# A three-block transformer on one core: projections of the second block from x times feature weights, the norm's factor per token applied later, key heads made once

## The reference

```python
def second_block(x, norm_g, w_in_a, sinks_a, w_in_b, w_out, final_g):
    for i in range(DEPTH_2):                       # 2 layers
        hn = rmsnorm_2(h, norm_g[i])               # x * rsqrt(mean(x^2) + 1e-5) * g
        q, k, v, z = split_proj(hn, w, n_kv)       # 16 query heads of 64; 2 or 4 key heads
        q, k = apply_rope(q, cos, sin), apply_rope(k, cos, sin)
        o = attention(q, k, v)                     # window of 128 with sinks; then causal
        o = o.reshape(B, S, MIX_WIDTH) * jax.nn.silu(z)
        h = h + o @ w_out[i]
    return rmsnorm_2(h, final_g)                   # goes to the third block's first FFN
```

## Time and profile before

| | us |
|---|---|
| runs | 2835.33, 2837.97, 2839.13 (median 2837.97) |
| the profiled execution | 2839.78 |
| its span | 2837.7 |
| PE busy | 2390.9 (84%) |
| DVE busy | 1238.6 (44%) |
| ACT busy | 935.7 (33%) |

### The profile page before, as it was taken

The page is one execution under the profiler, slowest core; times in us unless marked ns, Lnnn a source line. Parts: engine busy times, 40 slices in busy tenths (PEclk is TensorE's granted clock), DMA queues, the critical chain, the costliest instruction groups (busy, mean ns, idle before and its releaser), DMA issues.

```text
span 2837.7 us, 38160 instructions
## 1 busy us (share of the span) xinstructions
PE 2390.9 (84%) x16680; PEld 1711.8 (60%) x16680; DVE 1238.6 (44%) x1752; ACT 935.7 (33%) x1522; POOL 61.2 (2%) x36
## 2 busy tenths in 40 slices
PE   8999998666656565656889899999999999988998
PEld 8897784111211121111678778888788888967787
DVE  5567562000100011000475665467655656845654
ACT  5556541000000000000354554445443453733442
POOL 0000010000000000000000000000000000032000
PEclk9999999778887778777999999999999999999999
DMA  7553468999999999999524255474655554412552
GB/s 237 172 150 118 149 222 368 428 428 428 427 428 427 428 428 428 428 428 428 191 86 138 79 174 193 173 251 165 213 178 193 193 171 154 158 44 77 173 195 92
DMA packets 265894, 698.09 MB, mean 246 GB/s; under 512 B 32352, under 2 KB 208736, under 8 KB 239232
## 3 DMA queue, kind: packets, MB, share of 16 engines
q1 hardware_dynamic: 263424, 681.77, 63.5%
q0 software_dynamic: 2016, 13.67, 1.3%
q10 hardware_dynamic: 288, 0.22, 0.0%
HBM read 694.58 MB, written 1.05 MB: 245 GB/s over the span
## 4 chain that ended last, share of the span: by engine, by line
PE 60%; DMA 30%; DVE 7%; ACT 3%; issue 1%; DVEq 0%; ACTq 0%
PE ps L567 16%; PE ps L569 16%; PE ps L568 16%; DMA af<-in_w_exp_up 14%; DMA af<-in_w_exp_down 7%; DMA af<-in_w_exp_gate 7%; PE ps L1626 2%; PE ps L2396 1%; PE ps L860 1%; PE ps L1145 1%; PE ps L1656 1%; DVE ar L540 1%; PE ps L2016 1%; PE ps L992 1%; PE ps L1158 1%
## 5 line engine op out<-in xcount | busy, mean ns | idle before, releaser
L567 PE MATMUL ps<-ar 128*128 128x512 f32 (+1 forms) x2688 | 941.0, 350 | 28.1 <-DVE ar L1977 6.9
L569 PE MATMUL ps<-ar 128*128 128x512 f32 (+1 forms) x2688 | 923.0, 343 | 0.0
L568 PE MATMUL ps<-ar 128*128 128x512 f32 (+1 forms) x2688 | 922.7, 343 | 0.0
L540 DVE TENSOR_TENSOR ar<-af,ar 128x1024 fp32r<-128x1024 f32 x520 | 612.1, 1227 | 292.0 <-ACT ar L529 291.8
L567 PEld LDWEIGHTS ps<-ar 128*128 128x128 f32 x2688 | 514.5, 191 | 108.3 <-issue 11.8
L529 ACT ACTIVATE ar<-af 128x1024 fp32r<-128x1024 f32 x520 | 516.3, 1049 | 153.2 <-PE ps L569 152.8
L569 PEld LDWEIGHTS ps<-ar 128*128 128x128 f32 x2688 | 514.4, 191 | 59.0
L568 PEld LDWEIGHTS ps<-ar 128*128 128x128 f32 x2688 | 515.1, 192 | 55.7 <-issue 0.5
L1626 PE MATMUL ps<-af 128*32 128x512 f32 x2048 | 331.7, 782 | 220.9 <-DMA af<-in_w_exp_up 117.1
L1626 PEld LDWEIGHTS ps<-af 128*32 128x32 f32 x2048 | 64.3, 127 | 473.1 <-DMA af<-in_w_exp_up 190.7
L1656 PE MATMUL ps<-af 128*32 128x512 f32 x1024 | 163.9, 778 | 99.9 <-DMA af<-in_w_exp_down 87.7
(11 more groups left out here) (284 smaller groups left out, 1665.9 us busy)
## 6 DMA issues: line engine op xcount, KB each, us to landing
af<-in_w_exp_gate SPq DMA_DIRECT2D x64, 2048.0 KB, 41.1
af<-in_w_exp_up SPq DMA_DIRECT2D x64, 2048.0 KB, 40.9
af<-in_w_exp_down SPq DMA_DIRECT2D x64, 2048.0 KB, 41.4
af<-in_ffn_w_in SPq DMA_DIRECT2D x88, 1024.0 KB, 5.8
af<-in_ffn_w_out SPq DMA_DIRECT2D x44, 1024.0 KB, 5.2
af<-in_w_in SPq DMA_DIRECT2D x33, 1024.0 KB, 5.2
af<-in_sgu_w_in SPq DMA_DIRECT2D x16, 1024.0 KB, 7.3
af<-in_w_out SPq DMA_DIRECT2D x12, 1024.0 KB, 5.4
```

The costliest lines, as they stand in the source:

```text
L540: e.tensor_tensor(self.WL[load.pair][:, c], self.base(i)[:, c], f_(self.WH[load.pair][:, c]), ALU.subtract).then_inc(*self.dve.inc(("lo", ...
L567: e.matmul(o, lh, rh, start=start, stop=False, skip_group_check=True)
L568: e.matmul(o, lh, rl, start=False, stop=False, skip_group_check=True)
L569: return e.matmul(o, ll, rh, start=False, stop=stop, skip_group_check=True)
```

## The change

- **Feature weights first, the token's factor later.** The projections of both layers, and the gate and up projection of `ffn00`, take x times the norm's feature weights, rounded by ACT (`a_gained_hi`) and parted by DVE (`v_gained_lo`) chunk by chunk as the residual of each chunk is ready. The factor r is applied to sin and cos once per layer (so q and k get it with the rotation), to values per token (`t_columns` turns r into columns of tokens), to z before tanh, and in `ffn00` as scale of silu, in the product with up, and at the copy of x to tokens.
- **The first block's own norm** is not made before layer 0. Its weights are multiplied into layer 0's (`G20`), and layer 0's factor is taken from squares scaled by sqrt(g^2 + 1e-5) (`W20`) with eps 1e-11. The norm itself, needed for the residual, is made by DVE within attention 0 (`own_norm`), its sums by PE after q chunk 1.
- **Order.** The loads go q0, k, q1, v, q2, q3, z, o. Layer 0's first q chunk takes tiles in the order in which the residuals end. Chunk 1 of q is rotated before attention. ACT and DVE round and part the first two weight chunks before ACT copies `y` of expert 15.
- **Key heads once.** Heads are permuted on the host so that each half of the partitions meets its own key head in one tile: `wak` is one chunk instead of two, layer 0's keys one tile instead of two, layer 1's one chunk instead of two. `doubled` and its transfers of 256-byte pieces go.
- **Dummy matmuls**: 4 after expert 15 instead of 22 around the two norms; none after the layers, where there were 10 each.

```diff
-        doubled("wak", W1, 4096, 4)
+        columns("wak", W1, 4096, 256)
...
-            doubled("k%d" % l, src, 1024, nkv)
+            columns("qa%d" % l, src, 0, 256)
+            columns("k%d" % l, src, 1024, 64 * nkv)
+            columns("qb%d" % l, src, 256, 256)
             columns("v%d" % l, src, 1024 + 64 * nkv, 64 * nkv)
-            columns("q%d" % l, src, 0, 1024)
+            columns("qc%d" % l, src, 512, 512)
...
-        if q in (at["k0"], at["k0"] + 1):
-            return [self.pe.val(("ps", "y", 15))]
+        if q in (at["qa0"], at["k0"]):
+            return [self.pe.val(("raw", self.expert_last[4 * self.loads[q].pair]))]
...
+            if x == 15:
+                self.a_upto(e, self.at["k0"])
             for w in self.Aw.new(pe.val(("ps", "y", x)), *([pe.val(("ps", "moe%d" % (x - 2), 3))] if x > 1 else [])):
                 e.wait_ge(*w)
             e.activation(self.YE[x % 2], self.bank(("y", x)), ACT.Copy).then_inc(*act.inc(("ye", x)))
...
+    def a_gained_hi(self, e, name, src, hi, gain, j, ready):
+
+        for f in (2 * j, 2 * j + 1):
+            for w in self.Aw.new(*ready):
+                e.wait_ge(*w)
+            e.activation(hi[:, f, :], F(src)[:, f, :], ACT.Copy, scale=gain(f)).then_inc(*self.act.inc((name, "h", f)))
...
-        self.t_idle(e, 2, 6)
-        self.t_rms(e, "final1", self.B(9), KB, (0, 1, 4, 5, 2, 3, 6, 7))
-        self.t_idle(e, 2, 8)
-        self.t_rms(e, "norm20", self.B(9), KB)
-        self.t_idle(e, 2, 8)
+        self.t_idle(e, 2, 4)
...
+            if l == 0:
+                first_chunk("q0", self.at["qa0"], ready)
+                self.t_rms(e, norm, self.B(9), Ring(6), (0, 1, 4, 5, 2, 3, 6, 7))
+            else:
+                run(self.t_fm(e, "q" + n, 0, self.at["qa" + n], H, ready, DB, by_q,
+                              lambda: self.t_rms(e, norm, self.B(9), Ring(7), (6, 7), first=False)))
+            run(self.t_proj(e, "k" + n, 1, H, ready, DB, self.by_act("k" + n)))
+            rope("q" + n, F(self.qb), 0, ("out", "q" + n, 0), [])
+            run(self.t_fm(e, "q" + n, 1, self.at["qb" + n], H, ready, DB, by_q))
+            if l == 0:
+                self.t_rms(e, "final1", self.B(2), Ring(2))
+            rope("k" + n, kd, 0, ("out", "k" + n, 0), [])
+            self.t_columns(e, norm, Ring(6 + l))
+            run(self.t_proj_tm(e, "v" + n, 64 * nkv, H, ready, DB, self.by_act("v" + n)))
+            rope("q" + n, F(self.qb), 1, ("out", "q" + n, 1), [])
             self.end(self.pe, "att_in" + n)
...
+            e.tensor_tensor(self.sinS, self.C("sin"), self.RSTD, ALU.mult).then_inc(*dve.inc((norm, "sin")))
+            e.tensor_tensor(self.cosS, self.C("cos"), self.RSTD, ALU.mult).then_inc(*dve.inc((norm, "cos")))
...
+                    for f in range(8):
...
+                        e.scalar_tensor_tensor(out=F(self.x2)[:, f, :], in0=F(self.x)[:, f, :], scalar=self.V("final_norm_g", f), in1=self.SM2,
+                                               op0=ALU.mult, op1=ALU.mult).then_inc(*dve.inc(("final1", "o", f)))
...
+            def silu_z(e, name, c):
+
+                z = F(self.zb)[:, 2 * c:2 * c + 2, :]
+                for w in self.Vw.new(self.pe.val(("ps", name, c))):
+                    e.wait_ge(*w)
+                e.tensor_tensor(z, it(self.bank((name, c))), self.RSTD.unsqueeze(1).broadcast_to((P, 2, T)),
+                                ALU.mult).then_inc(*dve.inc(("scaled", name, c)))
+                if c:
+                    silu_last(name, c - 1)
...
+            def gained(c):
+                self.v_gained_lo(e, after, self.x2, lo, gain, c)
+                for f in (2 * c, 2 * c + 1) if l else ():
+                    e.tensor_scalar(F(self.B(6))[:, f, :], F(self.x2)[:, f, :], gain(f), None, ALU.mult).then_inc(*dve.inc((after, "u", f)))
+
+            def chunk(e, name, c):
+                residual(e, name, c)
+                if c:
+                    gained(c - 1)
```

More of the change, by code:

```diff
@@ L31, with by_head @@
 NVEC = sum(c for _, c in VEC.values())
+HEADS_OF = {2: [h for i in range(8) for h in (i, i + 8)], 4: [h for t in range(2) for a in range(4) for h in (8 * t + a, 8 * t + 4 + a)]}
+def by_head(a, nkv, axis):
+    n = a.shape[axis] // 16
+    order = np.concatenate([np.arange(h * n, h * n + n) for h in HEADS_OF[nkv]])
+    return np.take(a, order, axis=axis)
 def const_tables():
@@ L1700, in a_moe @@
         self.a_sqrt_table(e)
-        self.a_ahead(e, self.at["k0"] - 1)
+        for w in self.Aw.new(self.dve.val("gains2")):
+            e.wait_ge(*w)
+        e.activation(self.W20, self.W20, ACT.Sqrt).then_inc(*act.inc("w20"))
         self.end(act, "moe")
@@ L1836, in t_second @@
-            run(dense_q(0, 2))
+            ready, by_q = self.halves(norm), self.by_act("q" + n)
+            if l == 0:
[5 more added lines that the diff above has]
+            run(self.t_proj(e, "k" + n, 1, H, ready, DB, self.by_act("k" + n)))
@@ new lines, in a_second @@
+            q_out(e, "q" + n, 0)
+            self.a_sd(e, norm, 1e-5 if l else 1e-11)
+            self.a_ahead(e, self.at["k" + n])
+            self.a_copy(self.kd(nkv), tiles=nkv // 2)(e, "k" + n, 0)
+            self.a_ahead(e, self.at["qb" + n])
+            q_out(e, "q" + n, 1)
+            if l == 0:
+                for w in self.Aw.new(self.pe.val(("ps", "final1"))):
+                    e.wait_ge(*w)
+                e.activation(self.SM2, self.bank("final1")[:, 0:T], ACT.Sqrt, bias=self.EPS[1e-6]).then_inc(*act.inc(("final1", "sd")))
@@ L1905, in a_second @@
+            self.end(act, "layer" + n)
+            gained(3)
+            second = (self.at["ffn00.in"] + 1) if l else self.at["k1"]
+            self.a_hi(e, second, 0)
             self.a_sqrt_table(e)
-            self.a_square(e, after, self.x2, self.B(9), 3, [self.dve.val(("out", "o" + n, 3))])
-            self.a_hi(e, second, 0)
-            self.a_sd(e, after, 1e-5)
             self.a_hi(e, second, 1)
             self.a_next = second + 1
-        self.a_normed(e, "final2", self.B(6), self.XP3, ready=self.over("layer1"))
@@ L1951, in v_second @@
-            run(dense_q(0, 2))
-            self.end(dve, "att_in" + n)
-            def silu_z(e, name, c):
+            for w in self.Vw.new(dve.val((norm, "rstd"))):
+                e.wait_ge(*w)
+            e.tensor_tensor(self.sinS, self.C("sin"), self.RSTD, ALU.mult).then_inc(*dve.inc((norm, "sin")))
+            e.tensor_tensor(self.cosS, self.C("cos"), self.RSTD, ALU.mult).then_inc(*dve.inc((norm, "cos")))
+            for w in self.Vw.new(dve.val((norm, "cos"))):
+                e.wait_ge(*w)
@@ new lines, in v_second @@
+            self.v_ahead(e, self.at["k" + n])
+            rope("q" + n, F(self.qb), 0)
+            self.v_ahead(e, self.at["qb" + n])
+            rope("k" + n, self.kd(nkv), 0)
+            self.end(dve, "att_in" + n)
+            self.v_columns(e, norm)
+            self.v_ahead(e, self.at["v" + n])
+            for tt in range(2):
+                for w in self.Vw.new(self.act.val(("out", "v" + n, 0)), dve.val(("columns", norm))):
+                    e.wait_ge(*w)
+                e.tensor_scalar(vt[:, tt, :], vt[:, tt, :], self.SC[norm][:, tt:tt + 1], None,
+                                ALU.mult).then_inc(*dve.inc(*([("scaled", "v" + n)] if tt else [])))
@@ L2100, in a_third @@
         self.a_upto(e, self.at["ffn00.in"] + 1)
-        self.a_to_tm(e, "final2x", self.X)
+        self.a_sd(e, "final2", 1e-5)
+        for tt in range(2):
+            for w in self.Aw.new(self.pe.val(("ps", "final2x", tt, 0)), self.dve.val(("columns", "final2"))):
+                e.wait_ge(*w)
+            e.activation(self.X[:, tt, 0:512], self.bank(("final2x", tt, 0)), ACT.Copy,
+                         scale=self.SC["final2"][:, tt:tt + 1]).then_inc(*act.inc(("out", "final2x", tt, 0)))
         self.a_ffn(e, "ffn00")
```

320 lines of the change are left out of this document (195 added, 125 removed).

## The result

The changed kernel takes **2808.2 us** (median of 4 runs, 2806.9 to 2810.3) against 2836.8 us for the kernel before beside it (median of 4, 2835.3 to 2839.1): a ratio of 0.9902, 95% interval 0.9891 to 0.9913. A second group of runs gave 0.9911 (0.9897 to 0.9926). The forecast was 39.6 us less; 28.6 us is what came. The profiled execution took 2809.2 us for a span of 2807.2, 30.5 us less than the span of before.

A forecast was written before the change was run, and what follows sets the result against it. PE was taken to lead, with DVE close behind in attention and serial chains between stages. Savings 5.8 + 11.1 + 1.2 + 14.0 + 7.0 + 0.5 = 39.6 us gave 2798.5 us against the median 2837.97; range 2785 to 2814.

The forecast's parts named there:

- Part A: First block's attention: one doubled-key projection chunk instead of two, 48 matmuls fewer, 5.8 us saved and passed through the experts.
- Part B: Expert 15's evacuation to attention 0's first score: 39.1 us instead of 50.2, saving 11.1 us.
- The held evacuation: End of experts: ACT rounds weights before evacuating expert 15's `y`, delaying it 3.3 us, between 2 and 4.5.
- 10.5 us after the evacuation: Start of second block: layer 0's first q chunk done 10.5 us after expert 15's `y` is evacuated.
- Part C: Attention 0: net 1.2 us saved, between 6 us slower and 4 us faster.
- can both go: Attention 0: PE's 3.75 us rotation wait and the slow stretch worth 1.7 vanish; fifth score 3.6 us earlier.
- Rival 1: Attention stages: DVE becomes the bound, some 14 us of the gain are lost, 2812 us; chance 0.09.
- Part D: Layer 0 to attention 1: 27.5 us of PE work instead of 41.5, saving 14.0 us.
- Part E: Attention 1: rotation wait and slow stretches shrink, fifth score at 26.1 us; saves 7.0 us, between 3 and 9.
- Part F: Layer 1 to FFN: matmuls start 2.1 us earlier, a slow stretch takes 1.7 back; 0.5 us saved.
- Rival 2: Hand-overs at expert 15 and FFN: fewer dummies leave PE at half clock, costing up to 12 us, 2810; chance 0.09.

The follow-up runs named there:

- pairing_one: The kernel before with only the first block's doubled-key projection cut from two chunks to one; 2826.1 us, ratio 0.9972.
- y_first: The changed kernel with `y` of expert 15 evacuated ahead of the rounding of the first weights on ACT; 2806.3 us, ratio 0.9895.
- no_idle: The changed kernel without its four dummy matmuls ahead of the second block; 2807.8 us, ratio 0.9899.
- tanh_late: The changed kernel with ACT's tanh of a z chunk one step later, behind the copies for the values; 2801.4 us, ratio 0.9880.
- the doubled products: The changed kernel with the eight products of the first block's own norm done a second time on DVE in attention 0; 2813.3 us, ratio 0.9928.
- ffn_dummies: The changed kernel with ten dummy matmuls on PE ahead of the first FFN; 2801.5 us, ratio 0.9882.
- before_80: The kernel before with 40 dummy matmuls (80 records) added in the experts; 2833.0 us, ratio 0.9989.
- best: The changed kernel with `y_first`, `tanh_late`, `norm_early`, `ffn_dummies` and two dummy matmuls each in experts 5 and 9; 2787.4 us, ratio 0.9828.
- shift_28: The changed kernel with 14 more dummy matmuls (28 records), seven each in experts 5 and 9; 2799.5 us, ratio 0.9871.
- norm_early: The changed kernel with the first block's own norm finished before attention 0; 2802.7 us, ratio 0.9887.

## Why the prediction was right, and where it was not

The sign and the range held, and the sum was 11 us too large: the working missed by 5.1 us inside the parts it priced and by 5.5 in the third block, which it put at nothing; 1.6 us in the experts came unforecast, and that is luck; 1.9 more lie between the profiled executions (30.5) and the medians (28.6).

- **Part A** (5.8): 6.5 measured at the experts' first matmul, 6.9 in `pairing_one` (that point scatters over 2 us among the variants). Right, and passed on by the experts.
- **Part B** (11.1): 9.8. The held evacuation was forecast at +3.3 and measured at +3.1 (`y_first` took 2.8 of it back), for the reason given. The term that was mis-sized is the first q chunk, "10.5 us after the evacuation": 12.6 (1362.03 to 1374.6). I had it end with ACT's last rows. In the trace PE runs it without a gap from 1368.70, because the four dummy matmuls, which I left out, hold PE 1.8 us; `no_idle` gave 2.0 back. The scale by pointer cost what I took as the upper bound, 79 ns each (the row below, against 417 ns in the earlier trace rows); PE did not wait for it. The Trainium skill (ScalarE: Activation LUTs, What ACT_TABLE_LOAD costs) has about 93 ns; the trace agrees within 14.
- **Part C** (1.2): -0.8. Three steps failed. The end of the stage was priced at +1.9; the waits for L1032 are 2.16 and 2.98 us, against at most 0.8 before, and `tanh_late` took 3.3 back. "The moved norm is hidden there behind PE's q chunks" is wrong: the doubled products showed in full, and moving the norm gave 2.1. The fifth score came at 29.9, not 28.7. And of the wait for the rotation and the slow stretch behind it, which "can both go", only the wait by that name went: PE's transposes wait 2.35 us for DVE in its place (the row below), and the granted clock is 0.50 from 1425.8 to 1429.2 as it was for 3.5 us before. Rival 1 had the mechanism that an added microsecond of DVE shows; its 0.09 was too little for the stage, though its price (14 us) was too high. The sign set for it, DVE busy over 85% of the stage, did not come (58.3 of 72.1, 81%): it bound at less.
- **Part D** (14.0): 14.5. The walk gave 27.5 (its terms add up to 27.0 or, with the longer rotation wait, 27.6) against 27.0: here PE is the bound throughout, and such a sum held. No run takes this part alone; the row of the stage table is its evidence.
- **Part E** (7.0): 5.1. The fifth score is at 26.3 us, as walked (26.1), and both slow stretches, of 3.5 and 6.3 us, are gone. The miss is again the end, +0.8 forecast and 2.70 in one wait; `tanh_late` took 2.1 back.
- **Part F** (0.5): -0.6. PE starts the FFN 4.64 us after the last output matmul instead of 7.13, a gain of 2.5 (forecast 2.1); the slow stretch cost 2.3 us, not 1.7. The rest is a term that was left out: even at full clock the FFN's first 96 projection matmuls take 26.3 us (`ffn_dummies`), in before 25.5; the last square sums (L864) and the column transposes (L1857) now stand between them and take some 0.9 us.
- **Rival 2** (clock at the hand-overs) did not come at expert 15: the granted clock is 1.00 from 1368.7 to 1399.4. It came in front of the FFN. The same thing cost the 1.6 us of "FFN 0 and the SGU's first weights": a gap of 2.2 us for L542 (L540 in before) was followed by full clock in before, `pairing_one`, `before_80` and `best`, and by 3.4 us of half clock in after (from 1934.4) and in the other nine profiles of it and its variants.
- **The small matmuls of the third block** (0): -3.9, a cost that no edit of the change carries. The failed step is to take a stage with unchanged work as unchanged. `shift_28` shows that the number of PE instructions ahead can move it by 11.4 us; that it made just these 3.9 is likely and not shown, since `norm_early` took 118.3 with the same number as after, and the 118.0 of before is one profile.

PE's timeline of after in attention 0, then the group of its scaled copies by form, columns as in the earlier trace rows:

```profile
1424.64 0.55 PE L996 MATMUL ps<-cst,af 128*128 128x128 f32 x3 [2.35 <-DVE af L2014]
...
L1819 ACT ACTIVATE ar<-af,sm 128x256 fp32r<-128x256 f32 x8 | 3.6, 496 | 1.3 <-DVE af L1524 1.3
```

## What to carry to other kernels

When work is moved under cover, ask for the queue that it lands in, not for the busy share of its engine: DVE was busy 58 of 72 us in attention 0, and still 3.1 us more of it cost 3.5. An operation that waits for another engine should stand in its queue behind the copies that a third engine waits for; moving one tanh was worth 5 us. After any edit compare the stages that it does not touch as well, and before a small gain or loss is put down to it, try it with a few idle instructions more in an idle stage.

## What the runs showed of the hardware

- A stage of 64x64 matmuls took between 110.5 and 125.9 us for the same work, and the same within 0.1 us when one kernel ran twice. 14 dummy matmuls far ahead moved it by 11.4 us; 40 of them in another kernel by 3.6, which is no more than other edits did with the number unchanged (118.3 to 122.0).
- PE's instructions come in packets of 16 KB, one for some 127 matmuls with their weight loads. All 179 issue gaps over 0.4 us ended 1.2 to 1.6 us after such a packet had landed, and in this stage of very small matmuls the packets were 3.8 to 4.0 us apart in the median.
- The same gap of 2.2 us was followed by full clock in before and by 3.4 us of half clock in after, which cost 1.6 us: a single gap's cost cannot be read from the gap alone.
- Ten fp32 dummy matmuls in a 4.6 us gap kept the 2.4 GHz level and gave 2.3 us; four at a place where work was already waiting cost 1.8 to 2.0.
